# One-core decoder layer: attention for both key/value groups in one pass, with paired scores and the distances added by VectorE

## The reference

```python
s = jnp.einsum('bqkgd,bnkd->bkgqn', qc, k_cmp)           # compressed: 63 keys
s = s.astype(jnp.float32) - slopes[:, :, None, None] * dist
p_cmp = masked_softmax(s, dist >= 0)
imp = jnp.einsum('bkgqn,nj->bkqj', p_cmp, ov)            # importance of 16 key blocks
_, idx = lax.top_k(score, k_sel)                         # 8 blocks of 64 keys per query and group
...                                                      # selected: softmax over those blocks
mask = (dist >= 0) & (dist < WIN) & (spos[None, :] >= 0) # window: the last 256 keys
o = gc[..., 0:1] * o_cmp + gc[..., 1:2] * o_slc + gc[..., 2:3] * o_win
```

## Time and profile before

| | us |
|---|---|
| median of 3 executions | 1137.83 |
| the 3 executions | 1136.92, 1142.81, 1137.83 |
| span of the profiled execution | 1138.3 |

### The profile page before, as it was taken

One profiled execution on the slowest core, in us unless ns is written; L12 is line 12 of the kernel. 1 busy time (PEld: TensorE's weight loads), 2 busy tenths in 40 slices (PEclk: granted clock), 3 DMA queues, 4 the chain that ended last, 5 costly groups with the idle time before them and its releaser, 6 DMA issues.

```text
span 1138.3 us, 14739 instructions
## 1 busy us (share of the span) xinstructions
PE 1086.8 (95%) x4857; PEld 659.6 (58%) x4858; DVE 667.7 (59%) x1488; ACT 322.7 (28%) x800; POOL 174.1 (15%) x205
## 2 busy tenths in 40 slices
PE   6999999999999999999999899999958999999995
PEld 3544574444566787888787788555534444444442
DVE  2421223433353666677655379885567788887983
ACT  3311121111233545455444656323221000000000
POOL 0020221210000030000000040011103233333332
PEclk9999999999999999999999989999988999999998
DMA  6410042102000020000000050323447988899332
GB/s 243 114 42 0 1 94 72 37 1 91 1 2 3 3 77 3 3 3 2 2 1 1 3 184 2 123 111 111 165 187 261 337 286 297 314 385 346 114 102 84
DMA packets 74176, 119.77 MB, mean 105 GB/s; under 512 B 14368, under 2 KB 53376, under 8 KB 74120
## 3 DMA queue, kind: packets, MB, share of 16 engines
q1 hardware_dynamic: 63032, 88.08, 23.0%
q0 software_dynamic: 11088, 30.95, 7.9%
HBM read 105.90 MB, written 21.50 MB: 112 GB/s over the span
## 4 chain that ended last, share of the span: by engine, by line
PE 62%; DVE 7%; issue 2%; ACT 1%; POOL 0%; DVEq 0%; POOLq 0%; ACTq 0%
PE ps L1768 15%; PE ps L1120 10%; PE ps L1089 9%; PE ps L1778 8%; PE ps L1104 5%; PE ps L2091 5%; PE ps L1135 3%; PE ps L2101 2%; PE ps L1075 1%; PE ps L2122 1%; DVE big_u L2307 1%; DVE ring_down L2429 1%; PE ps L1094 1%; DVE big_u L1538 1%; PE ps L1422 1%
## 5 line engine op out<-in xcount | busy, mean ns | idle before, releaser
L1582 DVE STREAM_TRANSPOSE big_w<-big_w 32x256 f32<-32x256 f32 x384 | 167.2, 435 | 26.1 <-DMA big_w<-hn_dram,misc 19.8
L1768 PE MATMUL ps<-ring_gate_up,big_w 128*128 (+1 forms) x400 | 181.1, 596 | 0.0
L516 PE MATMUL ps<-big_w,big_u 128*128 128x512 f32 (+1 forms) x448 | 175.2, 546 | 0.1
L1243 DVE TENSOR_REDUCE big_w<-ps 128x2 f32<-128x768 f32 (+15 forms) x96 | 78.3, 815 | 106.6 <-PE ps L1094 87.1
L516 PEld LDWEIGHTS ps<-big_w,big_u 128*128 128x128 f32 x448 | 84.2, 192 | 76.6 <-issue 70.3
L1192 ACT ACTIVATE big_u<-ps 128x512 f32<-128x512 f32 (+7 forms) x160 | 75.7, 514 | 174.4 <-PE ps L1104 174.4
L1768 PEld LDWEIGHTS ps<-ring_gate_up,big_w 128*128 128x128 f32 x400 | 74.5, 191 | 84.3 <-issue 84.2
L1089 PE MATMUL ps<-ring_down,misc 97*128 97x512 f32 (+3 forms) x320 | 119.1, 481 | 2.0 <-ACT ring_gate_up L1202 2.0
L1120 PEld LDWEIGHTS ps<-ring_down,big_u 128*128 128x128 f32 x912 | 109.1, 192 | 15.5 <-issue 12.3
L1120 PE MATMUL ps<-ring_down,big_u 128*128 128x65 f32 x912 | 114.3, 274 | 0.9 <-ACT big_u L1192 0.9
L1183 ACT ACTIVATE big_u<-ps,big_w 128x384 f32<-128x384 f32 (+15 forms) x192 | 89.8, 527 | 7.8 <-DVE big_w L1243 6.4
(11 more groups left out here) (381 smaller groups left out, 1436.3 us busy)
## 6 DMA issues: line engine op xcount, KB each, us to landing
ring_gate_up<-in_w_gate SPq DMA_DIRECT2D x16, 1024.0 KB
ring_gate_up<-in_w_up SPq DMA_DIRECT2D x16, 1024.0 KB
ring_down<-in_w_down SPq DMA_DIRECT2D x16, 1024.0 KB
misc<-in_x SPq DMA_DIRECT2D x16, 512.0 KB, 3.5
big_w<-in_w_in SPq DMA_DIRECT2D x6, 1024.0 KB, 7.8
big_w<-in_w_out SPq DMA_DIRECT2D x8, 512.0 KB, 5.0
hn_dram<-big_u SPq DMA_DIRECT2D x8, 512.0 KB, 2.6
out<-ring_gate_up SPq DMA_DIRECT2D x8, 512.0 KB, 3.8
```

What stands on the lines that cost most here:

```text
L516: last = nc.tensor.matmul(ps[:, b, 0:width], uT[:, k, c * P:(c + 1) * P], wbuf[:, n % 2, k, 0:width], start=(k == 0), stop=(k == KD - 1))
L1243: ins = nc.vector.tensor_reduce(neg[:, br, h0:h0 + len(heads)], src, AX.X, ALU.max, negate=True)
L1582: last = nc.vector.transpose(dst[j * 32:(j + 1) * 32, :, i * 32:(i + 1) * 32], src[i * 32:(i + 1) * 32, :, j * 32:(j + 1) * 32])
L1768: last = nc.tensor.matmul(ps[:, 2 + b, :], xT[:, b, k, :], ring_gu[:, bass.ds(at + k * 2 * D_EXP, BANK)], start=(k == 0), stop=(k == KD - 1))
```

## The change

`attend` now works in 8 tiles of queries, both groups at once. The queries' and keys' 64 features of group 0 lie in partitions 0 to 63, those of group 1 in 64 to 127. A slot is some *pairs* of heads: head r of group 0 and head r of group 1. Each has its own score product of 64 rows, issued one behind the other into different banks. Slots: CMP one of four pairs, WIN two of two pairs (tile 0: one of four), SEL two of two for tiles 1 to 3 and four of one pair from tile 4. That makes 46. One set of banks (0 to 3) serves all slots, so slot j waits until VectorE has taken slot j - 1's scores.

Distance and mask rows and mask products are gone. VectorE adds a table of negated distances (-1e30 where masked) to the scores, scales by minus the slope, writes the result to SBUF and keeps its minimum, in one `tensor_tensor_reduce` a head (queries are divided by the slope in `project`). ScalarE takes the exponentials from SBUF, in place. From tile 4 on a bf16 product of 64 rows puts the selection's 0 or -1e30 into the bank first. The accumulators of both groups are banks 6 and 7, used by each group of work in turn; one read on VectorE serves all 8 heads.

On TensorE half of the value products of slot j - 2 (all, if it is CMP) stand ahead of the scores of slot j, the others between and behind the transposes of slot j - 1. On VectorE the selection and the queries stand ahead of the read.

```diff
@@ attend, tensor @@
-            if j >= 2:
-                pe.wait_ge(exp_done, j - 1)
+            if j >= 1:
+                pe.wait_ge(max_ready, heads_before[j])
...
+            for i, r in enumerate(pairs):
+                for at in range(0, n, BANK):
+                    w = min(BANK, n - at)
+                    if chosen:
+                        for g in range(NG):
+                            rows = slice(g * 64, (g + 1) * 64)
+                            nc.tensor.matmul(place(j, i, g)[:, at:at + w], sel_bias[rows, c % 2, :], key_hot[rows, at:at + w],
+                                             start=True, stop=False)
+                    for g in range(NG):
+                        rows = slice(g * 64, (g + 1) * 64)
...
+                        last = nc.tensor.matmul(place(j, i, g)[:, at:at + w], Q[rows, c % 4, r * P:(r + 1) * P], rhs,
+                                                start=not chosen, stop=True)
+                last.then_inc(scores_full, 1)
...
+        def values(j, a, b):
+            if a == 0:
+                if j == first_slot[br, c] and gi >= 1:
+                    pe.wait_ge(o_read, gi)
+                pe.wait_ge(wT_done, copies_before[j + 1])
...
         for j in range(J + 2):
+            n_v = len(blocks_of(j - 2)) if j >= 2 else 0
+            n_t = len(banks_of(j - 1)) if 1 <= j <= J else 0
+            v = n_v if n_v and slots[j - 2][1] == CMP else (n_v + 1) // 2
+            if v:
+                values(j - 2, 0, v)
             if j < J:
                 scores(j)
...
+            for k in range(n_t):
+                upto = v if k == 0 else v + (n_v - v) * k // n_t
+                if v < upto:
+                    values(j - 2, v, upto)
+                    v = upto
...
+                transposes(j - 1, k)
...
+            if v < n_v:
+                values(j - 2, v, n_v)
@@ attend, vector @@
+            for i, g, r in heads_of(j):
...
+                nc.vector.tensor_tensor_reduce(out=weights(j, i, g), in0=place(j, i, g), in1=table, scale=-SLOPES[h],
+                                               scalar=1.0e20, op0=ALU.add, op1=ALU.min,
+                                               accum_out=neg[:, br, h:h + 1]).then_inc(max_ready, 1)
...
         for j in range(J + 2):
             if j < J:
-                maxima(j)
+                scores_with_distance(j)
...
+            if j in select_at:
+                c, steps = select_at[j]
+                for step in steps:
+                    select(c, step)
+            for c, quarter in queries_at.get(j, ()):
+                queries(c, quarter)
             if j >= 2 and (j == J + 1 or slots[j - 2][0] != slots[j - 1][0]):
...
                 read_values(gi)
...
-            if j in select_at:
-                select(*select_at[j])
-            if j in queries_at:
-                queries(*queries_at[j])
```

More of the change, by code:

```diff
@@ L45 @@
 NEG = -1.0e30
-KR = 64 + 2 * N_BLK + 1
-ROW_SEL, ROW_ALIBI, ROW_SLOPE = 64, 80, 96
+CMP_COLS = 64
+WIN_KEYS = 3 * P
+SLOPES = [2.0 ** -(h + 1) for h in range(NH)]
 N_EXP = 16
@@ L235, in setup_memory @@
     M["q_rows"] = N.sem("query_rows")
-    M["s_alibi"] = [N.sem(f"alibi_loaded{i}") for i in range(4)]
     w = M["big_w"]
@@ L722, in _ @@
             nc.gpsimd.memset(M["v_win"][:, :, :, HD:HD + 1], 1.0).then_inc(pads, 1)
+            for h in range(NH):
+                last = nc.gpsimd.memset(M["unslope"][:, h:h + 1], 1.0 / SLOPES[h])
+            last.then_inc(pads, 1)
             o = Order(pool, u_sums)
@@ new lines, in transposes @@
+        def transposes(j, k):
+            if k == 0:
+                pe.wait_ge(exp_done, j + 1)
+            bank = transpose_bank(copy_use[copies_before[j] + k])
+            blocks = banks_of(j)[k]
+            for i in range(len(blocks)):
+                at = (j % 2) * 2048 + k * BANK + i * P
+                last = nc.tensor.transpose(ps[:, bank, i * P:(i + 1) * P], w_rows[:, at:at + P], ident[:, :])
+            last.then_inc(wT_full, 1)
+        def values(j, a, b):
+            gi, br, c, pairs = slots[j]
+            if a == 0:
+                if j == first_slot[br, c] and gi >= 1:
+                    pe.wait_ge(o_read, gi)
+                pe.wait_ge(wT_done, copies_before[j + 1])
+            blocks = blocks_of(j)
+            w = HD + 17 if br == CMP else HD + 1
+            for x in range(a, b):
+                g, r, blk = blocks[x]
@@ L1108, in values @@
-        def values(j):
-            gi, br, u, heads = slots[j]
-            c, g = u // NG, u % NG
-            if j == first_slot[br, u] and gi >= 2:
-                pe.wait_ge(o_read, gi - 1)
-            for k in range(2):
-                if copied_by[j][k]:
-                    pe.wait_ge(wT_done[k], copied_by[j][k])
-            w = HD + 17 if br == CMP else HD + 1
-            nb = len(key_blocks(br, c))
-            for i, (hl, h, b, n) in enumerate(blocks_of(j)):
-                v = v_cmp[0:n, g, 0:w] if br == CMP else vals[br][:, key_blocks(br, c)[b], g, :]
-                last = nc.tensor.matmul(ps[:, 6 + gi % 2, h * w:(h + 1) * w], weightsT(j)[0:n, i * P:(i + 1) * P], v,
-                                        start=(b == 0), stop=(b == nb - 1))
-            last.then_inc(pv_done, 1)
@@ new lines, in values, with selection, ssd_constants @@
+            if b == len(blocks) and b > a:
+                last.then_inc(pv_done, 1)
+        def selection(c):
+            pe.wait_ge(sel_ready, sel_count[c])
+            bank = transpose_bank(sel_use[c])
+            nc.tensor.matmul(ps[:, bank, 0:P], M["sel01"], identb[:, :], start=True, stop=True).then_inc(sel_full, 1)
+        def ssd_constants():
+            pe.wait_ge(dt_sem, 6)
+            bank = transpose_bank(prep_use)
+            nc.tensor.matmul(ps[:, bank, 0:64], tri[:, :], flat(1), start=True, stop=True)
+            nc.tensor.matmul(ps[:, bank, 64:128], ones, flat(1), start=True, stop=True).then_inc(prep_full, 1)
@@ L1291, in select @@
+                o.done(nc.vector.tensor_tensor(sc, sc, row(1), ALU.add))
                 o.mark(nc.vector.tensor_tensor(g3, si, sj, ALU.is_gt))
```

628 lines of the change are left out of this document (283 added, 345 removed).

## The result

The changed kernel takes 1159.3 us (median; 1158.2 to 1160.9), the kernel before 1137.5 beside it: 1.0178 times as long, 95% interval 1.015 to 1.0205. So it is slower, by 21.8 us where 7 were forecast. The profiled execution took 1160.5 us, its span is 1158.7.

What follows compares the result with a forecast made beforehand. TensorE bounds the attention stage: 340 - 4 - 82 + 14 + 56 + 11 + 2 = 337 us. Overall 1138.3 - 3 - 1.8 + 0.5 = 1134, with +11 for the clock 1145 us; range 1112 to 1172.

Steps and rivals of the forecast that it cites:

- The work: TensorE in the attention stage: paired scores (-49 us), masks (-19) and smaller savings, less the new selection bias, sum -82 us.
- The switches: TensorE going into 64-row products and out again in each of the 46 steps: +14 us, bounds 5 and 18.
- (c): Behind a window group, in the second selected slot, TensorE waits for VectorE's read after selection and queries: 20 us.
- (a): Behind a selected group, in the first window slot, TensorE waits 1.8 to 2.7 us for VectorE's read: 13 us for six.
- (b): Behind a compressed group, in the second window slot, TensorE waits 2.5 to 2.9 us for VectorE's read: 15.5 us.
- (d): Waits for VectorE's read in the first tiles, under z, and for the last group: 4 us.
- The copies: Values starting a step wait for the copy of the last transposes, 0.5 us in 22 steps: 11 us, bounds 5 and 15.
- The clock: Long TensorE waits in attention halve the granted clock 8 times, 1.4 us lost each: +11 us, bounds 0 and 20.
- B: Rival, chance 0.2: waits in attention as forecast, but TensorE's clock holds; 1134 us, no change.
- C: Rival, chance 0.22: VectorE starts score heads close together, waits hardly grow, switches cost 5 us; 1120 us.
- D: Rival, chance 0.1: VectorE's score instruction runs at half its rate, +27 us; 1172 us.
- E: Rival, chance 0.06: the paired 64-row score products on TensorE don't overlap; 1202 us.

Runs made afterwards that it cites:

- fill run: Changed kernel with 196 TensorE products that nobody reads filling each wait for a read that had over 1 us idle; 1128.5 us, ratio 0.990.
- half-filled run: Changed kernel with half as many products that nobody reads (99) in each of the 21 waits for the read; 1131.6 us, ratio 0.991.

## Why the prediction was right and wrong

The direction and the mechanism held; the time, 1145, was 14 us short. Over the stage as defined here the forecast was -68 (work) + 65 (idle time, 69 less the 4 that were there) + 11 (clock) = +8. The fill run takes the sum apart: work -65, idle time +57, clock +29.5, in all +21.4 (by the half-filled run some 3 us of the idle time belong to the clock). Against the forecast that is 3 us from the work, -8 from the idle time and 18.5 from the clock.

- **The work: right.** Sum -82 + 14 = -68; measured 276.5 us for 341.7, -65. The switches (taken at 0.3 us a step, 14 us) come out at 0.14 to 0.2 and 6.5 to 9, so the savings were some 73 us and not 82. The pairs' halving is shown by the run without it; the row that I took it from, L618, doesn't show it. Its eight records of 64 columns would take 0.215 us one behind the other at 0.42 ns a column, and took 0.29, and the program puts two neighbouring products on the same rows. That a pair costs one was right without evidence.
- **The waits for the read: mechanism right, size over.** 56 us forecast, 43.7 in the changed kernel. Case (c) is exact: six waits of 4.19, 4.66, 4.71, 3.42, 1.76 and 1.27 us make 20.0, forecast 20. Cases (a) and (b) were taken too long: 10.7 us for 13, and 9.3 for 15.5. Case (d) and the first weights were 3.7 for 7.5. One part of it is VectorE's head:

```profile
396.75 0.56 DVE L1245 CUSTOM_DVE_ANT_0 ring_gate_up<-ps,ring_down 128x384 f32<-128x384 f32 x1 [5.32 <-PE ps L1084]
397.23 0.08 DVE L1245 DVE_READ_ACCUMULATOR2_ANT big_w<- 128x1 f32 x1
397.23 0.55 DVE L1245 CUSTOM_DVE_ANT_0 ring_gate_up<-ps,ring_down 128x384 f32<-128x384 f32 x1
```

  Heads of 384 columns start 0.48 us apart, 0.09 beyond their columns, since the read of the minimum runs beside the next head; I took 0.2. Four heads are 1.9 us instead of 2.4. A smaller part is TensorE at half clock: it takes longer for the work ahead of the wait, so the wait is shorter. With the clock at 0.98, filled and idle time together are 55.5 us instead of 53.2.
- **The copies: right.** 7.3 us in 18 places, forecast 11 in 22. The wait for z was 2 us, here 0.4.
- **The clock: the step that failed.** Forecast 8 falls x 3.4 us = 27 us at half clock, 1.4 us lost in each, 11 us. Measured 88 us at half clock and 30 us lost. The price of a us at half clock was right (0.41 forecast, 0.34 measured); their number and length were not: in rows of 1 us the changed kernel has 16 stretches at half clock, of 3 to 10 us each, where I had 8 of 3.4. I had read two rows as a limit for one wait: 2.01 us held the clock, 2.92 us lost it. But the 2.01 us stood alone in a stage with 4 us of idle time. In the changed kernel waits of 1.0 us and more stand 5 to 33 us apart, the clock was down behind two of 1.69 and 1.89 us, and filling only the four long ones leaves 50 of the 88 us. The upper bound of 20 came from the same count, so it was no bound.
- **Elsewhere: as forecast, but not clear of noise.** The stage begins 2.1 us earlier (-1.8 forecast); in the other runs, with the same program up to there, it begins 0.2 to 3.1 us earlier than before.
- **The rivals.** B (clock holds, 1134): false by the profile; the kernel in which it is made to hold takes 1128.5. C (short waits): half true, the heads do start close together, but the reads average 2.1 us. D (half rate): false, 0.55 us for 384 columns. The Trainium skill, "Vector Engine (DVE) Microarchitecture Reference", section 7, names the halving for two SBUF sources that aren't bf16; no run here shows it, neither L869 with two such sources nor the score instruction with one in PSUM. E (no overlap): false.

## What to carry to other kernels

Put ahead of a step's first product for another engine only what can't wait behind it: work behind the scores covers VectorE's and ScalarE's answer, work ahead of them only delays it. Here the order of one engine was worth 72 to 76 us, and the place of one read on the other engine 34 or, under another order of TensorE, -27. And don't price idle time on TensorE by the length of one wait: a row of some busy neighbourhood in which a wait was harmless says nothing of the same wait among others. Filling waits with products that nobody reads is a cheap test of how much of a loss is clock; it gives a lower bound where the filling outlasts the wait.

## What the runs showed that I had not expected

- Waits of 1.0 to 2.4 us alone kept the clock at 0.93 in the stage; all 21 waits half filled left 0.98.
- A program with useless products (392 records) was 30.8 us faster than the same without.
- The chance of the clock is seen between executions: one program ran from 1078.9 to 1091.0 us, and its two profiled executions had stages of 296.2 and 289.7 us at clocks of 0.97 and 0.99.
- VectorE's read of the accumulated minimum, 0.08 us, costs nothing: the next head starts with it.
